# Gated linear attention on one core: a tile's two chunks issued side by side, and the output projection by token tiles

## What is computed

```python
att = jnp.where(causal, jnp.einsum('bhnid,bhnjd->bhnij', q_dec, k_inv), 0.0)
o_intra = jnp.einsum('bhnij,bhnje->bhnie', att, v)
upd = jnp.einsum('bhncd,bhnce->bhnde', k_to_end, v)
def step(state, inp):
    dec, u_n = inp
    return dec[..., None] * state + u_n, state
_, prev = lax.scan(step, init, (jnp.exp(b_last), upd))       # axes left out
o = o_intra + jnp.einsum('bhncd,bhnde->bhnce', q_dec, prev)
o = rms_norm(o, o_norm)
o = o * jax.nn.silu(g.astype(jnp.float32))
return o.astype(u.dtype) @ w_out
```

## Time and profile before

| | us |
|---|---|
| median of 3 runs (lowest, highest) | 1238.67 (1238.43, 1242.5) |
| the profiled execution | 1242.02 |
| its span | 1240.4 |
| PE busy in the span | 1143.4 (92%) |
| DVE busy | 390.9 (32%) |
| ACT busy | 283.1 (23%) |

### The profile page before, as it was taken

One profiled execution on the slowest core, in us unless ns is written; L12 is line 12 of the kernel. 1 busy time (PEld: TensorE's weight loads), 2 busy tenths in 40 slices (PEclk: granted clock), 3 DMA queues, 4 the chain that ended last, 5 costly groups with the idle time before them and its releaser, 6 DMA issues.

```text
span 1240.4 us, 18249 instructions
## 1 busy us (share of the span) xinstructions
PE 1143.4 (92%) x7733; PEld 682.1 (55%) x7733; DVE 390.9 (32%) x702; ACT 283.1 (23%) x459; POOL 203.8 (16%) x313
## 2 busy tenths in 40 slices
PE   6999997978999999996999997999969999999992
PEld 5688875863444344442678876777834444344430
DVE  3554236343111011013523346764242111011016
ACT  3533334120000000003222226763210000000002
POOL 1200040001212221113000004340011212221122
PEclk9999988988999999999899998999979999999996
DMA  8542003349999999995123210004289999999915
GB/s 296 153 151 83 32 1 120 118 171 330 389 397 395 392 392 402 407 370 198 42 102 102 87 50 1 1 1 170 85 282 391 389 396 397 393 393 411 400 42 203
DMA packets 92315, 283.24 MB, mean 228 GB/s; under 512 B 14088, under 2 KB 14256, under 8 KB 92256
## 3 DMA queue, kind: packets, MB, share of 16 engines
q1 hardware_dynamic: 72016, 239.32, 50.8%
q0 software_dynamic: 14272, 38.68, 9.3%
q10 hardware_dynamic: 5968, 4.40, 1.1%
HBM read 259.96 MB, written 22.41 MB: 228 GB/s over the span
## 4 chain that ended last, share of the span: by engine, by line
PE 80%; DVE 7%; issue 4%; POOL 4%; DMA 3%; ACT 2%; SPq 1%; POOLq 0%
PE ps L1685 42%; PE ps L1382 10%; PE ps L1384 9%; PE ps L1383 9%; PE ps L1629 3%; POOL xn_r L2067 1%; PE ps L1663 1%; DMA xn<-output_table,pos 1%; PE ps L1593 1%; PE ps L1528 1%; DVE h L1269 1%; DVE raw L1317 1%; DVE xn_r L1321 1%; POOL xn_r L2062 1%; POOL pad_r L2062 1%
## 5 line engine op out<-in xcount | busy, mean ns | idle before, releaser
L1685 PE MATMUL ps<-raw,s_f 128*32 128x256 f32 (+1 forms) x1536 | 180.9, 460 | 1.3 <-DVE s_f L1083 1.3
L1685 PE MATMUL ps<-w_f,s_f 128*32 128x256 f32 (+1 forms) x1536 | 175.6, 454 | 1.6 <-DVE s_f L1083 1.6
L1685 PE MATMUL ps<-xT_f,s_f 128*32 128x256 f32 (+1 forms) x1440 | 165.5, 454 | 0.0
L1685 PEld LDWEIGHTS ps<-raw,s_f 128*32 128x32 f32 (+1 forms) x1536 | 64.9, 120 | 110.6 <-issue 90.9
L1685 PEld LDWEIGHTS ps<-w_f,s_f 128*32 128x32 f32 (+1 forms) x1536 | 63.9, 118 | 107.5 <-issue 89.2
L1090 DVE TENSOR_TENSOR pad<-pad,ps 128x256 f32<-128x256 f32 x32 | 13.5, 421 | 338.1 <-ACT pad L718 338.1
L1685 PEld LDWEIGHTS ps<-xT_f,s_f 128*32 128x32 f32 (+1 forms) x1440 | 59.9, 118 | 95.7 <-issue 78.9
L1382 PE MATMUL ps<-w_hi,xT_hi 128*128 128x512 f32 x240 | 97.8, 408 | 9.5 <-DVE xT_lo L909 3.3
L1383 PE MATMUL ps<-w_lo,xT_hi 128*128 128x512 f32 x240 | 95.4, 398 | 0.0
L861 DVE SCALAR_TENSOR_TENSOR w_lo<-raw,gainT,w_hi 128x512 fp32r<-128x512 f32 x88 | 60.2, 747 | 111.7 <-ACT w_hi L536 111.7
L1384 PE MATMUL ps<-w_hi,xT_lo 128*128 128x512 f32 x240 | 95.4, 397 | 0.0
(11 more groups left out here) (283 smaller groups left out, 1517.0 us busy)
## 6 DMA issues: line engine op xcount, KB each, us to landing
xT_f<-in_m_w_down SPq DMA_DIRECT2D x36, 1024.0 KB, 11.7
w_f<-in_m_w_gate SPq DMA_DIRECT2D x32, 1024.0 KB, 10.8
w_f<-in_m_w_up SPq DMA_DIRECT2D x32, 1024.0 KB, 14.8
raw<-in_m_w_down SPq DMA_DIRECT2D x28, 1024.0 KB, 12.8
raw<-in_m_w_gate SPq DMA_DIRECT2D x18, 1024.0 KB, 4.9
raw<-in_m_w_up SPq DMA_DIRECT2D x18, 1024.0 KB, 7.0
xT_f<-in_m_w_gate SPq DMA_DIRECT2D x14, 1024.0 KB
xT_f<-in_m_w_up SPq DMA_DIRECT2D x14, 1024.0 KB
```

The costliest lines, as they stand in the source:

```text
L1685: ins = te.matmul(ps[rows * n:rows * (n + 1), bank + kind, 0:width // parts], stationary(k, kind), weights(k, parts, n), start=k == 0, sto ...
```

## The change

It does five things.

1. In the updates and in the between groups the loops over head and chunk are swapped: per head, the matmuls of chunk 2i and of chunk 2i+1 follow one another.
2. Four state buffers instead of two. The updates of the next tile are issued ahead of the between group of the tile before.
3. The copy of the transposed keys is halved between ACT and DVE, and ACT does it before the split of block 13. DVE copies attention blocks to `kinv` instead of `kT`, and so needs not wait for the transposes. DVE's split of block 13 moves behind the fourth state.
4. The output norm is done tile by tile, interleaved with the last states on DVE and with the squares on ACT.
5. The transposes of `o` are by token tile, and layer 0's projection starts with half(0, 0) when the first tile is ready; the order of the halves is (0,0) (1,0) (0,1) (1,1) (2,0) (2,1) (3,0) (3,1) where it was (0,0) (0,1) (1,0) (1,1) and so on.

```diff
-            se.copy(gate, ps[:, 0:4, :]).then_inc(A["ktok_out"], 1)
+            se.copy(gate[:, 0:2, :], ps[:, 0:2, :]).then_inc(A["ktok_out"], 1)
+            split(13)
...
+            o_squares(0)
+            o_squares(1)
+            o_first(0)
+            o_squares(2)
+            o_first(1)
+            tile_hi(1, 0)
+            o_squares(3)
+            o_first(2)
+            tile_hi(1, 1)
+            o_first(3)
+            tile_hi(1, 2)
+            tile_hi(1, 3)
...
+            dve.wait_ge(M["att_done"], NT)
+            att_out(0)
+            att_out(1)
+            dve.wait_ge(M["ktok_tr"], 2)
+            ve.tensor_copy(gate[:, 2:4, :], ps[:, 2:4, :]).then_inc(V["att_out"], 1)
+            att_out(2)
+            att_out(3)
...
+            for c in range(4):
+                state_of(c)
+            split(13)
+            o_mean(0)
+            state_of(4)
+            state_of(5)
+            gated(0)
+            o_mean(1)
+            state_of(6)
+            gated(1)
+            o_mean(2)
+            tile_lo(1, 0)
+            gated(2)
+            o_mean(3)
+            tile_lo(1, 1)
+            gated(3)
...
+            def updates(i):
+
+                chunks = [c for c in (2 * i, 2 * i + 1) if c < NCH - 1]
+                if i == 0:
+                    pe.wait_ge(A["ktok_out"], 1)
+                    pe.wait_ge(V["att_out"], 3)
+                else:
+                    pe.wait_ge(V["state_done"], GH * (chunks[-1] - 1))
+                for j in range(GH):
+                    for c in chunks:
...
+            updates(0)
+            within(0)
+            for i in range(1, NT):
+                updates(i)
+                between_chunks(i - 1)
+                within(i)
+            between_chunks(NT - 1)
...
+                if layer == 0:
+                    og_transposed(0)
+                    og_transposed(1)
+                    pe.wait_ge(A["o_squared"], GH * (NT - 1))
+                    half(0, 0)
+                    og_transposed(2)
+                    og_transposed(3)
+                    for j, n in ((1, 0), (0, 1), (1, 1)):
+                        half(j, n)
```

More of the change, by code:

```diff
@@ L174, in trunk @@
         v = region(8192, 4096).rearrange("p (i n) -> p i n", i=NT)
-        state = region(12288, 2048).rearrange("p (b h e) -> p b h e", b=2, h=GH)
+        states = [region(n, 1024).rearrange("p (h e) -> p h e", h=GH) for n in (12288, 13312, 2048, 3072)]
         reset = region(12288, T)
@@ L375, in h_halves, with out_halves @@
             return 2 * NT * layer + 2 * j + half + 1
+        def out_halves(layer, j, half):
+            at = 2 * half + j if layer == 0 and j < 2 else 2 * j + half
+            return 2 * (NT - 1) * layer + at + 1
         def panel_banks(p):
@@ L415, in last_banks, with tile_banks @@
             return psf[:, first:first + D]
-        XT = [0, NT, None, NT + KT]
-        def tile_banks(i):
-            return psf[:, 2048 + D * (i % 2):2048 + D * (i % 2 + 1)]
+        XT = [0, NT, None, 2 * NT]
+        def tile_banks(turn, i):
+            first = D * (i % 2) + (0 if turn == 1 else 2048)
+            return psf[:, first:first + D]
         def tile_of(t, i):
@@ L675, in _, with o_squares @@
             panel_out_tokens(6, 11, sg[:, :, BN:2 * BN], ACT.Silu)
-            split(13)
             se.preload_act_table_set(LN_EXP)
             act.wait_ge(M["ktok_tr"], 1)
-            se.copy(gate, ps[:, 0:4, :]).then_inc(A["ktok_out"], 1)
-            for i in range(NT):
+            se.copy(gate[:, 0:2, :], ps[:, 0:2, :]).then_inc(A["ktok_out"], 1)
+            split(13)
+            def o_squares(i):
                 act.wait_ge(M["inter_done"], 2 * i + 1)
@@ L1052, in gated @@
                 ins.then_inc(V["og_ready"], 1)
[L1054 to L1060, removed]
+            for c in range(4):
[14 more added lines that the diff above has]
+            gated(3)
+            tile_lo(1, 2)
+            tile_lo(1, 3)
             router_weights(0)
-            transposed_lo(1)
             split(14)
@@ L1602, in two_tiles @@
                     h_transposed_to(last, range(BK))
[L1604 to L1609, removed]
-                        if j:
-                            logits(j - 1, range(KT))
+                if layer == 0:
[7 more added lines that the diff above has]
+                        half(j, n)
+                    pe.wait_ge(V["xT_lo_done"], XT[1] + NT)
+                    h_transposed_to(0, range(KT))
+                    half(2, 0)
+                    logits(0, range(KT))
+                    h_transposed_to(1, range(KT))
+                    half(2, 1)
+                    logits(1, range(KT))
+                    half(last, 0)
+                    h_transposed_to(2, range(KT))
+                else:
+                    for j in range(NT):
+                        half(j, 0)
+                        if j:
+                            h_transposed_to(j - 1, range(KT))
+                        if j < last:
+                            half(j, 1)
+                            if j:
+                                logits(j - 1, range(KT))
                 half(last, 1, two_tiles)
```

120 lines of the change are left out of this document (55 added, 65 removed).

## The result

| | before | changed |
|---|---|---|
| median, same chip (us) | 1240.59 (1238.43 to 1242.72, 4 runs) | 1227.35 (1224.62 to 1228.91, 4 runs) |
| span of the profiled execution | 1240.4 | 1224.5 |

The changed kernel takes 0.9891 of the time (95% interval 0.986 to 0.9922), 13.2 us less by the medians. The forecast was 1228.2, with −10.5 against 1238.67.

The account below looks back on a forecast made before the run. PE, busy for 92% of the span, was taken as the bound, with DVE and ACT setting the pace around the norm. −8.45 + 4.1 − 9.1 + 2.9 = −10.5 against 1238.67 gave 1228.2 us, range 1223.8 to 1232.

Parts of the forecast that it names:

- Start: Before the recurrence: PE starts the updates at 166.95 instead of 167.80, through the halved key copy, −0.85 us.
- Clock in tile 0: Tile 0's groups: a 1.3 us wait instead of 2.16 leaves PE's clock at its upper level, −3.2 us.
- Pairs: Recurrence: alternating halves brings three update and three between groups to 1.92 us each, −5.55 us.
- New wait for state 1: Recurrence: tile 1's updates need state 1, so PE waits after tile 0's within group, +1.15 us.
- Projection: From og_ready to the third half's end: 15.4 us instead of 24.5, −9.1, including a 3.35 us wait for block 14.
- Clock after it: Projection: PE's clock falls to the lower level after the 3.35 us wait for block 14, +2.9 us.
- A: The forecast itself: early clock holds, late wait lowers it; 1228.2 us, range 1227 to 1229.5; chance 0.42.
- C: Clock still falls in tile 0, after two short waits; 1230.5 us, or 1227.6 if the late wait costs nothing; chance 0.20.
- B: Projection: the late wait does not lower the clock; 1225.3 us; chance 0.23.
- D: Recurrence: pairing gives nothing beyond present overlap, groups stay at 2.90 and 2.79; 1233.8 us; chance 0.07.
- F: Recurrence: alternation empties the array at each switch, +3.1 us for each of six groups; 1252 us, slower; chance 0.03.
- E: After the gain: it is handed back later, by late DVE or an expert load that doesn't move; 1233 to 1238; chance 0.05.

Follow-up runs that it names:

- e2: Kernel before with only the head and chunk loops swapped (pairs), still two state buffers and the old order otherwise; 1236.80 us, ratio 0.9972.
- e5: Kernel before, unchanged, profiled once more; 1240.24 us in one run.
- e9: Kernel before with the load of block 14 waiting for two finished tiles instead of four; 1240.26 us, ratio 0.9994.
- e1: Changed kernel with the loops of updates and between groups swapped back, so each chunk is issued whole; 1232.52 us, ratio 0.9936.
- e4: Changed kernel with the split of block 13 put back ahead of the key copies on ACT and DVE; 1231.94 us, ratio 0.993.
- e12: Changed kernel, unchanged, run once more; 1228.71 us, ratio 0.9893.
- e3: Changed kernel with the load of block 14 waiting for two finished tiles instead of four; 1224.11 us, ratio 0.9874.
- e11: Repeat of the changed kernel with block 14 loaded at two finished tiles; 1224.93 us, ratio 0.9877.
- e10: Changed kernel with block 14 loaded at two finished tiles and the old group order (updates, within, between per tile), four buffers kept; 1222.66 us, ratio 0.9851.

## Why the prediction was right

Right in sign and in the mechanism of the pairs, the waits and the load. The size of the gain was a fifth too small (10.5 against 13.2), with three terms off in the same direction, and one term, the clock in tile 0, was right for a reason that does not hold. By its steps:

- **Start:** −0.85 expected, 7.64 to 6.89 us into the stage, −0.75. The key copy in halves works; DVE's half ends last, as computed.
- **Clock in tile 0:** −3.2 expected and seen, in part by luck, because the reason given does not hold. I argued from the length of the wait alone (1.3 against 2.16). But e2 has 2.16 and no low clock; the kernel before has 2.16 and low clock in three profiles of three (with e5 and e9); e1 has the short wait with the chunks one after another and no low clock; e4 has a wait of 3.73 us with pairs and half the stretch. So the length of the wait alone does not decide, and pairs alone do not keep the clock up. The full 6.8 us occur only where a wait of 2.2 us is followed by groups that are issued one half at a time, and either change alone avoided them, in one profile each. That describes these profiles; a cause is not shown, and e2's median speaks for caution.
- **Pairs:** −5.55 expected. Groups of 2.00 and 1.95 us; e1 gives them back and loses 4.7 in the recurrence, 4.4 expected. The up to 2x of the Trainium skill (TensorEngine Tiling (Array Packing), § Overview) agrees with the trace only against two single groups in a row (twice 1.92 is 3.84, now about 1.9). Against the groups as they stood it was 1.5x, 2.90 to 1.93, because they overlapped already.
- **New wait for state 1:** +1.15 expected, 1.19 seen. The sum of the recurrence was −8.45; it is −8.41. The 0.2 us of slack for state 6 was enough: no further wait in the recurrence.
- **Tail to og_ready:** 10.4 us after the recurrence expected, 9.9 seen (189.21 to 199.14), +3.65 instead of +4.1.
- **Projection:** the wait for block 14 is there, between the second and third half, 2.70 instead of 3.35 us, because the load landed 5.0 us after its issue (ACT starts at 204.21), not 5.6.
- **Clock after it:** it fell, but for 3.4 us: 7.0 us for half(0,1) instead of 5.5, +1.45 where +2.9 was forecast. I took the length of the stretch from the two rows at hand, both 6.83. e1 and e4 had waits of 2.8 and 2.9 us and no low clock, e12 had it again; what decides between them stays open. That it fell at all was therefore not certain either.

These last three make 0.45 + 0.65 + 1.45 = 2.55 us, and −10.5 − 2.55 is −13.05; start and new wait give 0.14 back. The stage gave −12.9, and the medians of one chip −13.2. That the median came within 0.9 us of the forecast is partly luck: the baseline of 1238.67 was 1.9 below the one measured beside the changed kernel.

Of the rivals, A was right about both clock events in the changed kernel's two profiles. C's low clock in tile 0 occurred in neither; e4 has it, behind a longer wait. B's upper level behind the late wait occurred in e1 and e4. D and F (the pairs give nothing, or empty the array at each switch) are refuted by the groups and by e1. E did not occur: the rest of the kernel is 970.5 before and 969.5 after.

What the forecast missed is what the change left lying. The load condition had been free before (e9) and cost about 4 us now (e3, e11): 2.7 of wait, and the low clock behind it where it occurs. And the reordering of the groups, a part of its second point, cost 1.1 us of the stage instead of earning anything once there were four buffers (e10).

## What to carry to other kernels

When a stage is pulled forward, look at every wait that used to end under it, loads above all: a condition that was free can become the bound, and often it is wider than the data needs. Give the issue of small matmuls to the two halves of the array in turn, but take the gain from the group's present time, since neighbouring halves overlap in part already (2.90 us for a pair here, where two single groups would make 3.84). Test the parts of a change one by one even when the whole is faster; here one worked against the others. And when a profile's stage and the medians of many runs give different gains, as in e2, say so and leave the size open.

## What the runs showed of the hardware

- A pair of groups on the two row halves, 8 instructions of 256 columns each, takes 2.00 us alternated and 2.96 one half after the other; 8 alone take 1.99. On the column halves it is 1.95 and 2.86.
- The granted clock at the same place of the same kernel is reproducible at some places and not at others: 6.8 us low in tile 0 in all three profiles of the old recurrence, but 0, 3.4 or 6.8 us low at 47 to 56 us. The changed kernel's two profiled spans are 1224.5 and 1228.9; 3.1 of these 4.4 us come from 0 and 6.8 us of low clock at that one place (112.8 and 116.0 us from the matmuls at 45 us to the attention blocks), so a stage should be measured from its own start.
